# Experts in plain fp32 on column halves and quarters of the array, fed from twenty load buffers

## The reference, cut to what matters

```python
def swiglu(x, w13, w2):
    g, u = jnp.split(x @ w13, 2, axis=-1)
    return (jax.nn.silu(g) * u) @ w2

def moe_swiglu(xn, router_w, w13, w2):
    logits = xt @ router_w                       # xt: 256 x 1024
    top_vals, top_idx = lax.top_k(logits, 2)
    top_p = jax.nn.softmax(top_vals, axis=-1)
    ...
    for e in range(8):
        out = out + gates[:, e:e + 1] * swiglu(xt, w13[e], w2[e])
```

## Time and profile before

| | us |
|---|---|
| median of three runs | 1461.36 |
| the profiled execution, its own time | 1465.76 |
| its span, first to last instruction | 1463.9 |
| start of item 0's products | 534.0 |
| item 0 (128 rows) | 534 to 662 |
| first 64-row item | 662 to 762 |
| first 128-row item of the loop | 762 to 889 |
| last 64-row item | 1342 to 1447.4 |
| from its last product to the end | 1447.4 to 1464 |

### The profile page before, as it was taken

One profiled execution on the slowest core, in us unless ns is written; L12 is line 12 of the kernel. 1 busy time (PEld: TensorE's weight loads), 2 busy tenths in 40 slices (PEclk: granted clock), 3 DMA queues, 4 the chain that ended last, 5 costly groups with the idle time before them and its releaser, 6 DMA issues.

```text
span 1463.9 us, 20186 instructions
## 1 busy us (share of the span) xinstructions
PE 1352.4 (92%) x7603; PEld 1034.7 (71%) x7603; DVE 781.1 (53%) x889; ACT 646.1 (44%) x758; POOL 38.2 (3%) x53
## 2 busy tenths in 40 slices
PE   9999999999999998998879998788999878999685
PEld 6989888887988987785438886446886445887342
DVE  6576755545568588980018881007883006885003
ACT  6445544435445566760017771007772005774001
POOL 1000000000000000200000000000000000001000
PEclk9999999999999999999999999999999999999998
DMA  8837964553543438999999999999999999999995
GB/s 312 307 116 288 369 230 175 179 195 144 189 141 133 173 141 329 383 397 393 421 411 412 371 367 381 421 421 410 380 377 345 423 420 410 398 362 361 421 421 208
DMA packets 69696, 466.17 MB, mean 318 GB/s; under 512 B 7661, under 2 KB 9085, under 8 KB 16744
## 3 DMA queue, kind: packets, MB, share of 16 engines
q1 hardware_dynamic: 61976, 437.22, 76.1%
q0 software_dynamic: 7632, 27.69, 5.1%
HBM read 458.46 MB, written 19.01 MB: 326 GB/s over the span
## 4 chain that ended last, share of the span: by engine, by line
PE 71%; DMA 21%; DVE 5%; issue 2%; ACT 1%; SPq 0%; DVEq 0%; ACTq 0%
DMA raw<-in_moe_units 21%; PE bank L1504 20%; PE bank L1506 19%; PE bank L1505 19%; PE bank L1974 6%; DVE w_lo L889 1%; PE bank L1909 1%; ACT w_hi L532 1%; PE bank L1546 1%; PE bank L1592 1%; DVE w_lo L883 1%; PE bank L1713 0%; PE bank L1633 0%; PE bank L1696 0%; PE bank L1643 0%
## 5 line engine op out<-in xcount | busy, mean ns | idle before, releaser
L889 DVE TENSOR_TENSOR w_lo<-raw,w_hi 128x2048 fp32r<-128x2048 f32 x165 | 377.5, 2291 | 68.4 <-ACT w_hi L532 67.2
L1504 PE MATMUL bank<-w_hi,yT_hi 128*128 128x512 f32 x856 | 343.0, 401 | 21.9 <-DVE w_lo L889 20.6
L532 ACT ACTIVATE w_hi<-raw 128x2048 fp32r<-128x2048 f32 x165 | 316.1, 1916 | 82.5 <-PE bank L1506 64.5
L1506 PE MATMUL bank<-w_hi,yT_lo 128*128 128x512 f32 x856 | 337.0, 394 | 0.0
L1505 PE MATMUL bank<-w_lo,yT_hi 128*128 128x512 f32 x856 | 337.0, 394 | 0.0
L1974 PE MATMUL bank<-raw,pool_inv 128*64 128x256 f32 x1792 | 214.7, 385 | 44.5 <-DMA raw<-in_moe_units 39.8
L1974 PEld LDWEIGHTS bank<-raw,pool_inv 128*64 128x64 f32 x1792 | 140.6, 137 | 121.4 <-issue 85.3
L1454 DVE TENSOR_TENSOR qk<-qk,bank 128x256 f32<-128x256 f32 x28 | 11.8, 422 | 376.0 <-ACT qk L831 376.0
L883 DVE TENSOR_TENSOR w_lo<-raw,w_hi 128x1024 fp32r<-128x1024 f32 x160 | 188.1, 1219 | 41.4 <-ACT w_hi L526 40.0
L1504 PEld LDWEIGHTS bank<-w_hi,yT_hi 128*128 128x128 f32 x856 | 163.0, 190 | 60.5 <-DVE w_lo L889 24.7
L1506 PEld LDWEIGHTS bank<-w_hi,yT_lo 128*128 128x128 f32 x856 | 163.0, 190 | 35.1
(11 more groups left out here) (291 smaller groups left out, 1247.5 us busy)
## 6 DMA issues: line engine op xcount, KB each, us to landing
raw<-in_moe_units SPq DMA_DIRECT2D x336, 1024.0 KB, 9.2
raw<-in_layer_units SPq DMA_DIRECT2D x44, 1024.0 KB, 5.2
raw<-in_dense_units SPq DMA_DIRECT2D x33, 1024.0 KB, 5.8
sent<-in_x POOLq DMA_DIRECT2D x1, 6144.0 KB, 36.4
done<-in_x POOLq DMA_DIRECT2D x1, 6144.0 KB, 58.2
done<-qk POOLq DMA_DIRECT2D x4, 512.0 KB, 4.0
xn<-sent POOLq DMA_DIRECT2D x3, 512.0 KB, 9.1
x<-in_x SPq DMA_DIRECT2D x2, 512.0 KB, 4.0
```

What stands on the lines that cost most here:

```text
L532: act.activation(w_hi[:, st.split(u), :, :].rearrange("p a n -> p (a n)"), raw[:, st.slot(u), :], ACT.Copy)\
L889: dve.tensor_tensor(w_lo[:, st.split(u), :, :].rearrange("p a n -> p (a n)"), raw[:, st.slot(u), :], w_hi[:, st.split(u), :, :].rearrange( ...
L1504: pe.matmul(out, hi_l, hi_r, start=start, stop=False, skip_group_check=True)
L1506: return pe.matmul(out, lo_l, hi_r, start=False, stop=stop, skip_group_check=True)
```

## The change

**All items unsplit.** Items 0 to 3 hold 96 rows (`MID`), items 4 to 7 hold 64 (`FEW`), in this order. Item 0 is still expert 0. The 96 rows are three groups of 32, each on a quarter of the array's columns. The fourth quarter takes a share of the weight columns for all three groups, one group after another: in an up or gate step of 128 weight rows, quarters 0 to 2 take 384 columns each, quarter 3 three times 128. So a step is six products where a 64-row item has two. For w2, each 128 weight rows take nine products, 768 columns in every quarter. With hi and lo parts go the ACT and DVE instructions for `w_hi` and `w_lo` and the three passes of the experts; the dense stages keep them.

**Twenty buffers.** `slots` are the six `raw` buffers and fourteen laid over tiles that are no longer used. Each of the first 20 loads waits for its own tile (attention logits, layer units 19 to 21, the router's products), later ones for `units_read`, which TensorE raises after each unit.

**No DRAM for rows.** `gather` makes each item's transposed rows by a one-hot product (8 by 2 products of 96 or 64 columns) at step 6 of the item before. `back` multiplies the results, split into hi and lo, by a one-hot matrix and DVE adds them into `x` with the gate (`add_back`), at steps 1 and 2 of the next item. The one-hot matrices are laid out by `lay_out`, `spread_rows` and `select`. The fills of `sent` and `done`, the scatter, the fetches and the stores are gone.

**Code shape.** The eight items are written out one behind another on every engine. Items for overflow stand in a loop of six (`OVER`) with an `If` around a whole 96-row item:

```diff
-        with pe.If(n_items > NE):
-            item(NE, PAIRED + 1, over=True)
-            with pe.If(n_items > NE + 1):
-                item(NE + 1, PAIRED + 2, over=True)
-                ...
+        with pe.Fori(0, OVER) as k:
+            with pe.If(n_items > k + NE):
+                i = k + NE
+                pe.wait_ge(sem("added"), k * 4 + 4 * (NE - 1))
+                gather(i, True)
+                ...
+                item(i, over_units(k), True)
+                ...
             pe.nop()
-        pe.nop()
-
-        pe.wait_ge(sem("rows_sb"), 2 * NE + 2)
-        ...
+
+        pe.wait_ge(sem("y_sb"), NE)
+        pe.wait_ge(sem("spread"), NE)
+        back(NE - 1, False, range(4), spread, y_hi, y_lo, banks=(0, 2, 1, 3))
```

The same loop stands on ACT, DVE and SP. The new products:

```diff
+        def mid_up(w, k, b, start, stop):
+
+            a = (k % 4) * 512
+            for g in range(3):
+                r = slice(g * 32, (g + 1) * 32)
+                product(bank[b][r, 0:384], mid_x[:, k, r], w[:, a:a + 384], start, stop)
+            for g in range(3):
+                mm = product(bank[b][96:128, g * P:(g + 1) * P], mid_x[:, k, g * 32:(g + 1) * 32], w[:, a + 384:a + 512],
+                             start and g == 0, stop)
+            return mm
...
+        def mid_down(w, half, rows, block, start, stop):
+            ...
+            for g in range(3):
+                product(bank[4][g * 32:(g + 1) * 32, :], group(g), w[:, a:a + 512], start, stop)
+            for g in range(2):
+                product(bank[4][96:128, g * 256:(g + 1) * 256], group(g), w[:, a + 768:a + 1024], start and g == 0, stop)
+            for g in range(3):
+                product(bank[5][g * 32:(g + 1) * 32, 0:256], group(g), w[:, a + 512:a + 768], start, stop)
+            return product(bank[5][96:128, 0:256], group(2), w[:, a + 768:a + 1024], start, stop)
```

The loads, and what takes the place of the copies through DRAM:

```diff
+        room = [(f"free{units_from(MOE_BASE).slot(n)}", units_from(MOE_BASE).freed(n)) for n in range(RAW)]
+        room += [("logits", DEPTH * HEADS), ("xlogits_mm", DEPTH * XHEADS), unit_done(19)]
+        room += [unit_done(19)] * 2 + [unit_done(20)] * 2 + [unit_done(21)] * 4 + [("router_mm", 1)] * 3
+        ...
+        for u in range(ITEM_UNITS):
+            if u < RING:
+                hold(sp, *room[u])
+            else:
+                hold(sp, "units_read", item_units(0).room(u))
+            load_unit(item_units(0), u, moe[u])
...
+            def between(j):
+                if i and j == 1:
+                    pe.wait_ge(sem("spread"), i)
+                    back(i - 1, MANY[i - 1], (0, 1), spread, y_hi, y_lo)
+                elif i and j == 2:
+                    back(i - 1, MANY[i - 1], (2, 3), spread, y_hi, y_lo)
+                elif j == 3:
+                    if i:
+                        pe.wait_ge(sem("added"), i * 4)
+                    lay_out(i)
+                elif j == 6 and i + 1 < NE:
+                    gather(i + 1, MANY[i + 1])
```

More of the change, by code:

```diff
@@ L392, in _, with unit_done @@
         moe = io["moe_units"]
[L394 to L397, removed]
+        last = layer_stream(DEPTH - 1)
+        def unit_done(u):
+            return "unit_used", last.upto(u) + 2 * SPLIT
+        room = [(f"free{units_from(MOE_BASE).slot(n)}", units_from(MOE_BASE).freed(n)) for n in range(RAW)]
+        room += [("logits", DEPTH * HEADS), ("xlogits_mm", DEPTH * XHEADS), unit_done(19)]
@@ L399, in _ @@
         n_items = sp.value_load(info[0:1, 0:1], min_val=NE, max_val=ITEMS)
[L401 to L408, removed]
@@ L463, in _ @@
-            load_gain(l * 3 + 4, io["mix_norm_g"][l + 1] if l + 1 < DEPTH else io["final_norm_g"])
[L465 to L511, removed]
@@ L1451, in few_item @@
-        def few_item(i):
-            for j in range(ITEM_STEPS):
-                dve.wait_ge(sem("silu"), i * ITEM_STEPS + (j + 1) + NT * DENSE_TURNS)
-                dve.tensor_tensor(hid[:, 0, 0:2 * P], hid[:, 0, 0:2 * P], bank[j % 2][:, 0:2 * P], ALU.mult)\
-                    .then_inc(sem("hid_ready"), 1)
-        item(0, 0, first=True)
-        with dve.Fori(0, PAIRED) as p:
-            few_item(p * 2 + 1)
-            item(p * 2 + 2, p + 1)
-        few_item(NE - 1)
+            of_items(gate8[:, :, :], gate[:, :, :])
@@ new lines, in add_back, with gated @@
+        def add_back(i, col, which):
+            for n in which:
+                t, half = n // 2, n % 2
+                s = slice(half * 512, (half + 1) * 512)
+                dve.wait_ge(sem("back_mm"), i * 4 + (n + 1))
+                dve.scalar_tensor_tensor(x[:, t, s], bank[6 + half][:, :], gate[:, t, col:col + 1], x[:, t, s],
+                                         ALU.mult, ALU.add).then_inc(sem("added"), 1)
+        def gated(i, j, many):
+            n = 3 if many else 2
+            dve.wait_ge(sem("silu"), i * ITEM_STEPS + (j + 1) + NT * DENSE_TURNS)
+            dve.tensor_tensor(hidden[:, 0:n * P], hidden[:, 0:n * P], bank[j % 2][:, 0:n * P], ALU.mult)\
+                .then_inc(sem("hid_ready"), 1)
@@ L1901, in _, with lay_out, back_part @@
-        gs = (xgT_hi, xgT_lo)
-        def item(i, o, then=None, first=False, over=False):
-            st = item_stream(i)
+        def lay_out(i):
+            pe.wait_ge(sem("places"), i + 1)
+            pe.matmul(bank[7][:, 0:T], ones, places[:, :, :].rearrange("p t r -> p (t r)"), start=True, stop=True)\
+                .then_inc(sem("places_mm"), 1)
+        def back_part(out, one_hot, hi_part, lo_part, start, stop):
+            pe.matmul(out, one_hot, hi_part, start=start, stop=False, skip_group_check=True)
+            return pe.matmul(out, one_hot, lo_part, start=False, stop=stop, skip_group_check=True)
@@ new lines, in product, with few_up @@
+        def product(out, rows, moving, start, stop):
+            return pe.matmul(out, rows, moving, start=start, stop=stop, skip_group_check=True)
+        def few_up(w, k, b, start, stop):
+            for col in range(2):
+                mm = product(bank[b][col * FEW:(col + 1) * FEW, 0:256], few_x[:, k, :],
+                             w[:, (k % 4) * 512 + col * 256:(k % 4) * 512 + (col + 1) * 256], start, stop)
+            return mm
[7 more added lines that the diff above has]
+                             start and g == 0, stop)
+            return mm
@@ new lines, in item, with arrived, up @@
+        def item(i, units, many, between=None):
+            one_up, one_down = (mid_up, mid_down) if many else (few_up, few_down)
+            def arrived(u):
+                slot = units.slot(u)
+                pe.wait_ge(sem(f"in{slot}"), units.landed(u))
+                return slots[slot]
+            def up(u, b, turn_j=None):
+                for m in range(2):
+                    if m and turn_j is not None:
+                        turn_hidden(turn_j)
+                    w = arrived(u + m)
+                    for k in range(4 * m, 4 * m + 4):
+                        mm = one_up(w, k, b, k == 0, k == KD - 1)
+                    mm.then_inc(sem("units_read"), 1)
@@ L1935, in item, with down @@
-            if over:
-                turn_rows(i)
-            pe.wait_ge(sem("gather_lo"), o * 2 + 1)
-            up(st, 0, lambda: pe.wait_ge(sem("gather_lo"), o * 2 + 2), FT, gs, (0,))
-            up(st, 2, None, FT, gs, (2,))
+            def down(u, j, m):
+                w = arrived(u)
+                for half in range(2):
+                    block = 2 * m + half
+                    mm = one_down(w, half, hT[:, j % 2, :, :], block, j == 0 and block == 0,
+                                  j == ITEM_STEPS - 1 and block == 3)
+                mm.then_inc(sem("units_read"), 1)
@@ L2020, in _ @@
-        item(0, 0, turn_few_rows, first=True)
-        with pe.Fori(0, PAIRED) as p:
-            few_item(p * 2 + 1, p, turn_rows)
-            item(p * 2 + 2, p + 1, turn_few_rows)
-        few_item(NE - 1, PAIRED)
+                down(e + 5, j - 1, 1)
+                if between is not None:
+                    between(j)
+            pe.wait_ge(sem("turned"), i * ITEM_STEPS + ITEM_STEPS)
+            down(ITEM_UNITS - 2, ITEM_STEPS - 1, 0)
+            down(ITEM_UNITS - 1, ITEM_STEPS - 1, 1)
```

700 lines of the change are left out of this document (304 added, 396 removed).

## The result

The changed kernel takes **1418.5 us** (median of 4 runs, 1418.3 to 1420.6), the kernel before 1463.0 (4 runs, 1460.2 to 1465.5). The ratio is 0.970, 95% interval 0.9677 to 0.9722: 3.0% less, where 1.1% less (1445 us) was forecast. The time lies in the range 1402 to 1497, near rival 1 (1413). The profiled execution took 1418.5 with a span of 1416.7. Times and ratios in this document leave out two executions in a slower state, one of `gate` (1705.4) and one of the kernel before (3418.8).

A forecast was written before the change was run, and what follows sets the result against it. 128-row items were taken as bound by three passes, 64-row items by loads. Last product 1397.9 plus 37.1 of loop plus 12.5 gave span 1447.5; plus 1.9 less 4.4, 1445 us, 8-in-10 range 1402 to 1497.

The forecast's parts named there:

- rival 1: PE's overflow loop at the end: jumps are cheap, held in the instruction buffer, 5 us in all; time 1413; chance 0.27.
- First product: Start of the experts: gather starts at 532.0, takes 2.8 us, two ACT copies follow, first product at 535.9.
- Quarters: Products of 96-row items: all four quarters run at once, an up step takes 0.65 us, a unit 2.61.
- rival 2: Up steps of 96-row items: quarters hold each other up, 0.76 us a step instead of 0.65; time 1495; chance 0.24.
- 96-row item: Items 0 to 3: 121 us each, bound by PE, over the 104.6 us of their loads; DMA share about 0.87.
- rival 3: 96-row items not slower than their loads, 112 us or less, loads bind throughout; time 1387; chance 0.07.
- 64-row items and buffers: Items 4 to 7: 82 us of PE work, twenty buffers full at first, 151 loads at 2.49 us, last product 1397.9.
- Fills: Removing the 6 MB fills beside the dense layer: taken as 0 gain, up to 29 us if PE waited for loads there.
- The end: PE's loop of six over the overflow body after the last product: eleven jumps of 3.475 us, 38.2 us, 37.1 after the last product.
- Rest of the end: From last product to kernel end without the loop: 16.5 us less two idle stretches of PE, leaving 12.5.

The follow-up runs named there:

- gate: The changed kernel with one more If around the loop over overflow items on PE, SP, ACT and DVE: 1413.9 us, ratio to before 0.965.
- ring6: The changed kernel with six buffers instead of twenty, overflow ring six instead of fourteen: 1454.4 us, ratio to before 0.9928.
- ring12: The changed kernel with twelve buffers instead of twenty, overflow ring six instead of fourteen: 1439.0 us, ratio to before 0.983.
- fills: The changed kernel with the two 6 MB DRAM fills put back in layer 0, nothing waiting for them: 1419.5 us, ratio to before 0.969.
- turns12: The changed kernel with TensorE's loop over overflow items run through twelve times instead of six: 1424.8 us, one run.
- two_ifs: The changed kernel with a second, never entered copy of the If and its body in each turn of TensorE's overflow loop: 1426.5 us, one run.
- order_ring6: The changed kernel with 96-row and 64-row items by turns and six buffers instead of twenty: 1439.3 us, ratio to before 0.9822.

## Why the prediction was wrong in its size, and where it was right

- **First product** forecast 535.9, measured 535.3, but partly by luck: the gather began at 530.5 where I had 532.0, and took 3.8 us where I had 2.8, since a record of 96 columns cost as much as one of 128. The turns of `idle_turns` took 0.65 us for four quarters, as costed.
- **Quarters: right.** The step was priced at 0.65 us with all four quarters at once. Up units (48 streams each; the "96 records" of the prediction count the weight loads too) start at 719.86, 722.47 and 725.05, 2.61 and 2.58 us apart (2.61 forecast, 3.0 in rival 2), as this timeline of PE shows:

```profile
719.86 2.83 PE L1861 MATMUL bank<-raw,mid_x 128*32 128x384 f32 x48
722.47 2.84 PE L1861 MATMUL bank<-slot_bias,mid_x 128*32 128x384 f32 x48
725.05 2.77 PE L1861 MATMUL bank<-slot_qk,mid_x 128*32 128x384 f32 x47
```

- **96-row item** forecast 121, measured 118.2 for item 0 and 121.7 to 121.8 for the others. Two parts were off and offset each other: `gather` 3.8 us for 2.8, the seven groups of transposes 0.48 each, 3.4 together, for 4.1. Rival 2 (from 125.1 on) and rival 3 (112 or less) both fall by this. The DMA share beside them is 0.95 where I wrote 0.87; the rate, 42 MB in 121.7 us, is as it must be, so the busy share does not fall in proportion to a rate below the top.
- The Trainium skill, *TensorE: Matmul & The Clock Gate*, part 3, gives 2.38 for three column tiles. The trace here, with four quarters, shows no such loss: a step takes the 0.65 us that its 2 x 384 columns cost at the halves' 0.85 ns.
- **64-row items and buffers: right.** First item 82 forecast, 83.8 measured; 1.3 of the difference is `gather` (3.8 for 2.5). The 151 loads left at 2.49 us gave 1397.9 for the last product; measured 1398.3, with 150 loads left at 1018.55 and 2.52 us for each. ring6 and ring12 show that in this order each buffer is worth about one load.
- **Fills: right**, 0 by the run `fills`.
- **The end: this step failed.** The prediction put "11 x 3.475 = 38.2 us", 37.1 of it exposed, on the loop of six. Measured: one branch of 3.58 us and ten of 0.21 to 0.26, 7.05 us exposed. The mechanism of rival 1 held, at 7.0 instead of its 5, the rest being 0.3 us of other sequencer work a turn.
- **Why it failed.** The earlier trace rows hold only jumps to code that PE did not have: 3475 ns to code it had never run, 5952 and 6008 back to the start of a body after all of that body had been executed. I took both as the price of a far jump. The eleven jumps of the loop have only two targets between them, and skip the body. `turns12` and `two_ifs` show that the price belongs to the first visit, when the code is fetched. The row that spoke for it, SP's 45 ns, I set aside because SP's body is small.
- The Trainium skill, *Advanced Engine Details and Errata*, section Control Flow Timing, gives about 108 ns for a compare-and-branch. Here returning jumps took 0.21 to 0.26 us and first visits 3.4 to 4.7, so neither agrees, but the returning ones are within a factor of 2.4. The branches of SP, ACT and DVE in the changed kernel took 0.04 to 0.07 us.
- **Rest of the end**: 12.5 forecast, 18.4 - 7.05 = 11.4 measured; what the 1.1 us are was not looked for.

In the sum: of the 30.8 us between the forecast span of 1447.5 and the measured 1416.7, 30.0 come from the loop's exposed cost (37.1 - 7.05) and 1.1 from the rest of the end, while 0.4 go the other way at the last product. The median came out 26.5 under the forecast, since here the profiled execution was typical, and I had taken off 4.4 us for one that was not.

**Where the 44.5 us came from.** `order_ring6` is the change (its products, its rows by TensorE, its code shape) in the order and with the number of buffers of before: 26.0 us less than before (1465.3), with the loop's 7 us in it. Putting the 96-row items first costs 15.1 us at six buffers (1439.3 to 1454.4). Fourteen more buffers give 35.9 back (to 1418.5). The sum is 46.8, from 1465.3 to 1418.5; the 44.5 are from 1463.0, and the 2.3 between lie in the times of the kernel before. In the other sequence, with twenty buffers, the order costs 42.6. So the part of this change that loses most is the order (the loop loses 4.6): it gathers the product-bound items at one end and the load-bound ones at the other, where twenty buffers can carry only twenty units of slack across, once.

## What to carry to other kernels

When some stages are bound by products and others by loads, alternate them: buffers then carry slack across every boundary, and the limit becomes the larger of the two sums instead of a sum of maxima. A buffer more was worth one load (2.5 us) with a single boundary from product-bound to load-bound work, and about three (7.3 us, from six to twelve) where there were four. Between twelve and twenty it was one load in both orders; that it is worth nothing once a pair is covered, no run here shows. Price a far jump by whether the code at its target is still held: count first visits, and returns behind much other code (6 us in the earlier trace rows), not jumps.

## What the runs showed of the hardware that was not expected

- PE's sequencer returned to any of three places, with a body of some 3,700 instructions between neighbours, in 0.20 to 0.26 us; a first visit took 3.39 to 4.66 us (`gate`, `two_ifs`).
- Four column quarters of fp32 products, 12 load and stream pairs in 0.65 us, ran for 120 us at a time at the price of the halves, 0.85 ns a column and record.
- A product on the full width of the array that streamed fewer columns was no cheaper: the 32 records of a `gather` took 3.8 us with 96 and with 64 streamed columns, as with 128 in the earlier trace rows (3.81).
- Loads reached 420 GB/s beside them, no less than beside halves.
- A jump's price need not stand in its branch record. SP's loop in the changed kernel:

```profile
L463 SPq COMPARE_BRANCH  x6: 50/50/55, 1371.6 to 1380.2; - x6
```

```profile
L462 SPq COMPARE_BRANCH  x6: 40/45/50, 1377.1 to 1380.6; - x6
```

SP's first jump over its body is recorded with 55 ns at 1371.6, but its next instruction starts 5.4 us after it; the turns that follow take 0.7 us each. That this too is a fetch was not tested. It costs nothing here, since the last load had been issued. The first jumps of ACT and DVE, over smaller bodies, took 50 and 73 ns, with the next instruction 0.5 and 0.2 us after they began.
